# Two value projections computed as one product of two by two blocks with seven block products, and attention items placed later and closer together

## The reference, cut to what matters

```python
proj = einsum('bld,dn->bln', x, w_in) + b_in          # x: (1, 512, 1024)
qa, fa, ia, za, qb, kb, vb, zb, qi, ki, wi, ga, gb = split(proj)
oa = hgrn2_mix(qa, fa, ia, lb)                        # recurrence; ia are its values, 512 wide
ua = (rms(oa) * norm_a_g * silu(za)) @ w_up_a
ob = dsa_mix(qb, kb, vb, qi, ki, wi, rel_bias)        # indexer, top 128 keys per query, softmax; vb are its values, 512 wide
ub = (ob * silu(zb)) @ w_up_b
merged = sigmoid(ga) * ua + sigmoid(gb) * ub
y = merged @ w_out
out = layer_norm(ALPHA * x + y, ln_g, ln_b)
```

## Time and profile before

| | |
|---|---|
| median of 3 runs | 460.01 us |
| the 3 runs | 454.6, 460.01, 460.18 us |
| the profiled execution, its own time | 454.26 us |
| its span, first to last instruction | 452.4 us |
| granted TensorE clock | 0.997 of full speed |

### The profile page before, as it was taken

The page is one execution under the profiler, slowest core; times in us unless marked ns, Lnnn a source line. Parts: engine busy times, 40 slices in busy tenths (PEclk is TensorE's granted clock), DMA queues, the critical chain, the costliest instruction groups (busy, mean ns, idle before and its releaser), DMA issues.

```text
span 452.4 us, 7707 instructions
## 1 busy us (share of the span) xinstructions
PE 444.5 (98%) x2946; PEld 363.5 (80%) x2946; DVE 308.3 (68%) x586; ACT 237.1 (52%) x399; POOL 172.7 (38%) x171
## 2 busy tenths in 40 slices
PE   9999999999999999999999999999999999999994
PEld 7778888888888878888878887888788888778883
DVE  4546589999999855246889994891370057887676
ACT  5745445253236745384958656844594273335431
POOL 0444432583168822673006010000055453055955
PEclk9999999999999999999999999999999999999998
DMA  8808122257022794203221995022039354235013
GB/s 264 297 12 294 72 91 94 93 139 233 1 92 46 178 373 152 66 29 99 88 95 23 220 260 152 3 96 94 0 100 374 113 185 169 91 146 220 0 46 139
DMA packets 17859, 59.26 MB, mean 131 GB/s; under 512 B 2616, under 2 KB 4448, under 8 KB 16352
## 3 DMA queue, kind: packets, MB, share of 16 engines
q1 hardware_dynamic: 17008, 54.39, 35.7%
q0 software_dynamic: 576, 4.19, 4.7%
q10 hardware_dynamic: 240, 0.20, 0.1%
HBM read 54.57 MB, written 10.50 MB: 144 GB/s over the span
## 4 chain that ended last, share of the span: by engine, by line
PE 93%; DVE 4%; ACT 1%; issue 1%; POOL 0%; DVEq 0%; POOLq 0%
PE bank L641 22%; PE bank L642 22%; PE bank L643 22%; PE bank L974 3%; PE bank L971 3%; PE bank L973 3%; PE bank L804 2%; PE bank L789 2%; PE bank L887 2%; PE bank L840 2%; PE bank L780 1%; PE bank L779 1%; PE bank L931 1%; PE bank L769 1%; PE bank L768 1%; PE bank L685 1%
## 5 line engine op out<-in xcount | busy, mean ns | idle before, releaser
L1972 POOL TENSOR_TENSOR w_lo<-w_raw,w_hi 128x512 fp32r<-128x512 f32 x72 | 94.7, 1341 | 141.7 <-ACT w_hi L982 141.7
L641 PE MATMUL bank<-x_hi,w_hi 128*128 128x512 f32 x336 | 133.0, 396 | 0.0
L642 PE MATMUL bank<-x_lo,w_hi 128*128 128x512 f32 x336 | 131.2, 390 | 0.0
L643 PE MATMUL bank<-x_hi,w_lo 128*128 128x512 f32 x336 | 130.9, 390 | 0.0
L641 PEld LDWEIGHTS bank<-x_hi,w_hi 128*128 128x128 f32 x336 | 63.1, 188 | 13.9 <-issue 0.8
L643 PEld LDWEIGHTS bank<-x_hi,w_lo 128*128 128x128 f32 x336 | 63.1, 188 | 13.6
L642 PEld LDWEIGHTS bank<-x_lo,w_hi 128*128 128x128 f32 x336 | 63.1, 188 | 12.2
L982 ACT ACTIVATE w_hi<-w_raw 128x1024 fp32r<-128x1024 f32 (+2 forms) x63 | 62.3, 1011 | 3.3 <-PE bank L643 1.7
L1704 DVE TENSOR_TENSOR w_lo<-w_raw,w_hi 128x512 fp32r<-128x512 f32 x44 | 28.1, 683 | 27.9 <-ACT w_hi L982 27.9
L1069 ACT ACTIVATE prob<-prob,nmax 128x128 f32<-128x128 f32 (+3 forms) x32 | 17.7, 555 | 41.6 <-DVE nmax L1524 41.5
L1500 DVE MAX8 best<-score 128x8 f32<-128x256 f32 (+2 forms) x48 | 26.8, 559 | 1.1
(11 more groups left out here) (269 smaller groups left out, 808.5 us busy)
## 6 DMA issues: line engine op xcount, KB each, us to landing
w_raw<-in_w_units SPq DMA_DIRECT2D x58, 512.0 KB, 5.0
out_t<-in_w_units POOLq DMA_DIRECT2D x2, 1024.0 KB, 11.2
out_t<-out_t POOLq DMA_DIRECT2D x2, 1024.0 KB, 10.4
z_b<-out_t SPq DMA_DIRECT2D x2, 1024.0 KB, 5.8
y_sb<-in_x_tok SPq DMA_DIRECT2D x4, 512.0 KB, 5.2
out<-y_sb SPq DMA_DIRECT2D x8, 256.0 KB, 2.0
x_raw_hi<-in_x_t SPq DMA_DIRECT2D x4, 256.0 KB, 5.1
x_raw_lo<-in_x_t SPq DMA_DIRECT2D x4, 256.0 KB, 5.8
```

The lines of the kernel that those rows point to most:

```text
L641: nc.tensor.matmul(dst, a_hi, b_hi, start=first, stop=False)
L642: nc.tensor.matmul(dst, a_hi, b_lo, start=False, stop=False)
L643: return nc.tensor.matmul(dst, a_lo, b_hi, start=False, stop=last)
L1972: nc.gpsimd.tensor_tensor(split_target(u, kiwi_lo, x_lo, w_lo)[:, k, :], raw(u)[:, k, :], split_target(u, kiwi_hi, x_hi, w_hi)[:, k, :].bi ...
```

## The change

The weights of vb (512 columns) and ia (512 columns) together are a 1024 by 1024 matrix. It is cut in two by two blocks of 512 by 512, x in two by two blocks (tokens by rows of the weights), and the product is made in seven block products instead of eight, with sums of x blocks and sums of weight blocks. The seven block units (`VI_BLOCKS`: b11, b21, t1, t2, t3, t4, b22) take 24 matmuls each, in two quarters, one a bank; they replace vb0, vb1, ia0 and ia1. Each block's weights are 1 MB. There are now 34 units and 122 quarters instead of 31 and 124.

The new starts are zb0 12, b11 16, b21 18, zb1 20, t1 24, za0 26, t2 30, za1 32, t3 36, qb0 38, t4 42, kb0 44, b22 48, qb1 50, kb1 54, fa0 58, fa1 62, qa0 66, qa1 70, ga0 74, gb0 90, up0 106. A bank of a block unit is left in the step behind its quarter.

- DVE makes four sums of x blocks (`sum_x`, four operations of 128 by 1024) directly behind the split of x; ACT rounds them (steps 13, 25, 26, 27), DVE makes the lo parts (steps 15, 26, 28, 30).
- SP copies four weight blocks in DRAM: those of t1 and t3 behind the constants at unit 3, that of t2 behind the load of unit 4, that of t4 behind the load of unit 5. POOL issues the four adding DMAs in steps 12, 13, 17 and 22. The load of a sum waits for it.
- `leave_block` combines the banks: 18 DVE operations of 128 by 512 in place of 8.
- Top k rounds of block 3 start at step 39 at 1.3 a step. Items 0 to 15 stand at steps 50 to 59, three pairs in four steps, items 16 to 31 at 61 to 70. The recurrence is 6 steps later (`Q_PREP` 70, `Q_TREE` 79 and 89), `Q_MERGE` is 100.
- The sigmoids of gb0 and gb1 move into step 100 of ACT (two of 128 by 1024). The loads of the output blocks b11 and b21 move from SP's place before up0 to that before up2. The lo parts of qa0 and qa1 move from DVE to POOL, those of gb2 and gb3 from POOL to DVE.

```diff
-UNITS = ["kiwi", "qi0", "qi1", "zb0", "zb1", "za0", "za1", "qb0", "kb0", "vb0", "vb1", "qb1", "kb1",
-         "ia0", "ia1", "fa0", "fa1", "qa0", "qa1", "ga0", "ga1", "ga2", "ga3",
+UNITS = ["kiwi", "qi0", "qi1", "zb0", "b11", "b21", "zb1", "t1", "za0", "t2", "za1", "t3", "qb0", "t4", "kb0",
+         "b22", "qb1", "kb1", "fa0", "fa1", "qa0", "qa1", "ga0", "ga1", "ga2", "ga3",
          "gb0", "gb1", "gb2", "gb3", "up0", "up1", "up2", "up3"]
...
+VI_BLOCKS = ("b11", "b21", "t1", "t2", "t3", "t4", "b22")
+QUARTERS = [2 if n in VI_BLOCKS else 4 for n in UNITS]
+STARTS = [sum(QUARTERS[:u]) for u in range(NMAIN + 1)]
...
-Q_ITEM = [39 + 2 * (i // 2) if i < 16 else 55 + 4 * ((i - 16) // 2) // 3 for i in range(len(ITEMS))]
-Q_ATTEND = [Q_ITEM[4 * (i // 4) + 3] + (4 if i < 16 else 3) for i in range(len(ITEMS))]
+Q_ITEM = [(50, 61)[i // 16] + 4 * (i % 16 // 2) // 3 for i in range(len(ITEMS))]
+Q_ATTEND = [Q_ITEM[4 * (i // 4) + 3] + 3 for i in range(len(ITEMS))]
...
+VI_SUMS_AT = {12: "t1", 13: "t3", 17: "t2", 22: "t4"}
+X_HI_AT = {13: 0, 25: 1, 26: 2, 27: 3}
+X_LO_AT = {15: 0, 26: 1, 28: 2, 30: 3}
...
-    for b, first, per in ((1, 18, 1.7), (2, 28, 1.7), (3, 38, 1.5)):
+    for b, first, per in ((1, 18, 1.7), (2, 28, 1.7), (3, 39, 1.3)):
...
+                if UNITS[u] in OUT_SUMS and a == 0:
+                    sp.wait_ge(sum_done[UNITS[u]], 16)
+                sp.dma_start(w_raw[:, u % 2, c], unit_source(u)[:, c]).then_inc(w_in[u % 2][a], 16)
...
+                    begin_sum("t1")
+                    begin_sum("t3")
                     sp.wait_ge(table_done, 1)
                     sp.dma_start(t5_row, table[:]).then_inc(row_out, 16)
...
+                if u == 4:
+                    begin_sum("t2")
                 if u == 5:
+                    begin_sum("t4")
                     sp.wait_ge(row_out, 16)
...
+            def quarter_block(u, i):
+
+                name = UNITS[u]
+                wait_bank(u, i)
+                first = name != "b21"
+                if i == 0 and name in X_OF:
+                    pe.wait_ge(s_lo_done, X_OF[name] + 1)
...
+                for j in range(PAIRS):
+                    if i == 0:
+                        wait_lo(pe, u, j + 1)
+                    a_hi, a_lo = vi_stationary(name, j, i)
...
+            def leave_block(name, i):
+
+                bank, v_low, a_up = proj_bank[i][:], v_b[:, 2 + i, :], v_a[:, i, :]
+                if name == "b11":
+                    ins = nc.vector.tensor_tensor(v_low, bank, bias_vb[:], ALU.add)
...
+                elif name == "t3":
+                    link(nc.vector.tensor_tensor(v_a[:, 2 + i, :], a_up, bank, ALU.subtract))
+                    ins = nc.vector.tensor_tensor(v_low, bank, v_low, ALU.add)
...
+            def sum_x():
+
+                a11, a12, a21, a22 = (x_part(r, h) for r in range(2) for h in range(2))
+                nc.vector.tensor_tensor(xs_raw[:, 0], a21, a22, ALU.subtract).then_inc(s_raw_done, 1)
+                dve.wait_ge(s_raw_done, 1)
+                nc.vector.tensor_tensor(xs_raw[:, 1], xs_raw[:, 0], a11, ALU.subtract).then_inc(s_raw_done, 1)
+                nc.vector.tensor_tensor(xs_raw[:, 2], a11, a21, ALU.subtract).then_inc(s_raw_done, 1)
+                dve.wait_ge(s_raw_done, 2)
+                nc.vector.tensor_tensor(xs_raw[:, 3], a12, xs_raw[:, 1], ALU.add).then_inc(s_raw_done, 1)
...
+            sum_x()
             dve.wait_ge(early_in, 32)
...
+            def add_vi_block(name):
+
+                second = OUT_SUMS[name][1]
+                pool.wait_ge(vi_begun[name], 16)
+                if second in OUT_SUMS:
+                    pool.wait_ge(sum_done[second], 16)
+                nc.gpsimd.dma_start(vi_sums[name], vi_block(second), accum_op=ALU.add,
+                                     max_dma_last_dim=8192).then_inc(sum_done[name], 16)
```

291 lines of the change are left out of this document (187 added, 104 removed).

## The result

The changed kernel takes 483.65 us (median of 4 runs, 481.06 to 484.49), the kernel before 457.42 beside it: a ratio of 1.056, 95% interval 1.047 to 1.066. On another chip it was 482.05 against 454.9, 1.057 (1.052 to 1.063). The forecast was 465, range 452 to 475. In the profiled executions the span went from 452.4 to 482.1 us, +29.7, where the sum of the prediction said +7.9.

The account below looks back on a forecast made before the run. PE was taken to bound the kernel, with DVE near to late. Terms -5.4 + 2.1 + 7.0 + 4.2 = +7.9 on 454.26 give 462.2; seen from the middle of two run levels, 465 us was forecast, range 452 to 475.

Parts of the forecast that it names:

- Part 1, matmuls: Four units of 48 matmuls become seven of 24, 192 to 168 on PE: 5.4 us less.
- Part 2, sums of x: Four early DVE sums, held by POOL's lo pieces, delay PE's unit 2: 2.1 us more, between 0 and 3.2.
- Part 3, banks: DVE leaves banks late for PE at steps 20, 25, 32, 38, 44 and 49: 7.0 us together, 0 to 9.
- step 20's 0.9: PE waits 0.9 us before step 20 for b21's bank, left behind DVE's adds and rounds.
- Steps 44 and 49 ... 0.8 and 0.3: PE waits 0.8 and 0.3 us there for banks that DVE leaves late, with rounds and q or k banks.
- Part 4, DMAs: Copies and additions delay zb1's load; ACT holds step 18's relus behind it, PE waits near 61 us: 4.2 us.
- its upper case (9.3): t2's addition also runs ahead of zb1's load, 5.1 us more: 9.3 us in all.
- I take 4.2: The size chosen for the DMA stall before step 20, between nothing and 9.3 us.
- Part 5, the rest: Items, POOL's added lo pieces, ACT's sigmoids in step 100 and later steps: 0, with at most 2 us for items or sigmoids.
- The second rival: Early DMAs hold ACT for long, with sums of x at 3.2: +13 to +16 us, 468 to 476; chance 0.28.
- The checks named: PE gaps of 0.9 before step 20, 2.3 within t1, about 1.6 before za1; unit 2 after 22.12; ACT behind unit 6's DMA.

Follow-up runs that it names:

- e15: e12 with the score adds of step 23 moved to step 34 and the top k rounds laid out again: 455.15 us, ratio 0.997.
- e4: Changed kernel with the four sums of x in DVE's steps 8 to 11, one a step: 478.74 us, ratio 1.055.
- e1: Changed kernel with the recurrence's lower bound back at its old steps (DVE 36 and 40, ACT 37): 478.41 us, ratio 1.052.
- e14: e12 with the lower bound alone put back as in the changed kernel (DVE step 47, ACT step 48): 465.70 us, ratio 1.020.
- e3: Changed kernel with the adding DMA for t3 issued in POOL's step 26 instead of 13: 477.33 us, ratio 1.049.
- e12: Changed kernel rearranged: table, adding DMAs, sums of x, their lo parts, lower bound, rounds, t2's subtractions and step 23's score adds moved: 458.82 us, ratio 1.004.
- e7: Kernel before with only the four copies and four adding DMAs added, into arrays that nothing reads: 463.75 us, ratio 1.016.
- e2: Changed kernel with the shifted bias table's DMA issued behind zb1's load instead of ahead of it: 475.88 us, ratio 1.044.
- e9: Changed kernel with ACT rounding zb1's halves behind the relus of steps 18 and 19, no DMA moved: 481.01 us, ratio 1.059.
- e6: Changed kernel with rounds, lower bound, shifted table, additions for t2, t3, t4 and sums of x all moved: 475.76 us, ratio 1.043.

## Why the prediction was wrong

**What bounds the kernel.** Right: PE sets the end, and DVE's banks are what is nearest to late. All but two of the eleven waits shown are released by DVE.

**Part 1, matmuls: right.** In e15 PE's busy time is 4.2 us less.

**Part 2, sums of x: right in size** (2.25 for 2.1) and in the hold: two of the four took 2.3 us beside POOL's pieces. That it adds to the rest was not: e4 took it away and lost it again in step 14.

**Part 3, banks.** Right where it counted: 2.6, 2.2, 2.0 and 1.0 us for 2.3, 1.7, 1.0 and 0.8, with the releasers named; step 20's 0.9 lay under the DMA stall. The step that failed is "Steps 44 and 49 ... 0.8 and 0.3". For step 49 I counted rounds and banks and left out that the lower bound hangs on the first item's step: 8.1 us, 7.9 of them given back by e1 and 6.6 taken again by e14 at these steps. That DVE was late in step 36 before was the cover that hid the wait.

**Part 4, DMAs.** Mechanism and place were right, ACT held behind zb1's first half; the size was not, 13.2 for 4.2 (and 0.9 for b21's bank). The failing step is the sum over volume that puts the first half at 60.7, or at 65.8 in its upper case (9.3), and the choice "I take 4.2". The half landed at 69.6, since each small packet of the table waited for a large one, and t2's addition came ahead of the load too; how much of the lateness is t2's, no run separates. So the relus came at 70.56, 8.8 us later than I counted. From them to PE's step 20 it was 6.0 us where I counted 4.4, since the adds took 2.89 us beside POOL's pieces: 1.6 more. Step 20 at the lower clock makes 2.2. Against that, step 20 was due 4.4 us later than before, for the losses ahead of it, so that much of the lateness cost nothing. The sum had neither the hold nor the clock.

**Part 5, the rest.** 0 was wrong by 3.8: adding DMAs issued among POOL's lo pieces make the score adds beside them wait (step 14: 1.4 us with two DMAs, 0.5 with one in e3, none in e12, where the DMA is issued behind the pieces, 1.5 in e7 with the DMAs alone), and small gaps in steps 16 to 18, 86 and 113 to 118, whose cause I didn't test. The prediction priced an adding DMA by its volume and its issue on POOL at nothing.

**Rivals and range.** The second rival (DMAs at their worst, 468 to 476) was the nearest. No case had a stall of more than 0.3 us between steps 44 and 94, or the low clock, so the range ended at 475.

**The checks named.** The gaps stood at the named places: 2.3 (with its step 2.5) for 2.3 within t1, 1.3 for 1.6 before za1, unit 2 at 24.37, ACT behind the load of unit 6. None of them named step 49.

Open: why the gain of e2, e3 and e9 in the profiled gaps (9 to 12 us) is only partly in their medians (6 to 8, 5 to 6, 1 to 3 below those of the changed kernel). In each profile 3.6 to 4.3 us more were lost between steps 24 and 31, over half of it at the lower clock. Longer executions of one kernel tend to show a lower mean clock (e2: 472.24 us at 0.990, 480.27 at 0.976), so such stretches are a part of the difference; what they waited for was not profiled.

## What to carry to other kernels

When items of a hand-written order move, list every constant that is derived from theirs, down to the smallest operation: a wait for one exp on 128 by 4 values cost 8 us, because work that was late before had hidden it. Where an engine is 93% busy (84.5 of 90 us on DVE in the kernel before, 83.4 in e15), work taken from another engine may bring nothing until that one's order is laid anew: here 24 matmuls less, with more work for DVE and the queues, gave +26 us, and a time level with the kernel before once the rounds, adds and lo parts had been moved. Issue POOL's DMAs behind its runs of pieces, or where DVE has no operation with two SBUF inputs, and keep small-packet transfers out of the time of large-packet ones if something waits behind them in the queue.

## What the runs showed of the hardware that I had not expected

- A DVE operation with two SBUF inputs beside a run of POOL's lo pieces can wait for the whole run, not for one piece: 5.52 us for 1.22, 4.34 for 0.69, 5.54 for 1.60 (two adds), each ending 0.5 to 1.1 us after POOL's run (94.77, 113.89, 91.80). What these have in common is a DMA that POOL issues. In all traces of this case 18 such DVE operations took over 3 us, and each began at most 0.9 us after POOL had issued an adding DMA, with lo pieces behind it. Beside lo pieces without a DMA issue none took over 2.4 us, which is a hold of about one piece. e7 against the kernel before differs by the DMAs alone: 5.61 us against 1.33. It is the issue on POOL and not the traffic: e12 makes the same copies but issues t1's addition behind the pieces, and step 14 loses nothing there. Why the issue does this, no run shows. The Trainium skill, SBUF — State Buffer, section "Who interferes with whom", says that such an operation contends with a GpSimd one that reads SBUF and that the order of issue decides who blocks; the rows agree on who is held, and show that the turn need not come between two pieces.
- Two DMA queues at work took turns packet for packet, 261 to 251, though one moved 5 times the bytes; 1 MB took 29.9 us in place of 9.7.
- After PE had been idle for 5.2 us (the changed kernel, up to 174.50) its clock was 0.50, the lower level, for the whole step behind it, which took 2.6 us more; e6 shows the same behind a wait of 4.2 us in step 42. Behind waits of 2.3 us it went both ways: 1.00 in the changed kernel (98.50), 0.50 for 3.4 us in e3 (86.3 to 89.7, 1.6 us more). The prediction priced idle time at its own length.
